# Attention with heads paired on row and column halves, both key tiles projected first, and GpSimd scaling the exponentials by the inverse of their sum

## What is computed

```python
ql, kl, vl = split(xl @ w_qkv + b_qkv)         # 16 heads of 64; 4 key/value heads
ql, kl = apply_rope(ql), apply_rope(kl)        # latents only
for each block of 128 queries:                 # 4 blocks
    keys  = [context 256, window of +-128 around the block]
    logits = (q . k) * 64 ** -0.5, masked to |distance| <= 128
    m = max(max(logits), sink)                 # one sink logit per head
    p = exp(logits - m)
    o = (p / (sum(p) + exp(sink - m))) @ v
```

## Time and profile before

| | us |
|---|---|
| median of three runs | 2054.65 |
| lowest and highest | 2053.88, 2057.94 |
| the profiled execution | 2064.9 |
| its span | 2063.1 |
| TensorE busy | 1968.5 (95%) |

### The profile page before, as it was taken

One profiled execution on the slowest core, in us unless ns is written; L12 is line 12 of the kernel. 1 busy time (PEld: TensorE's weight loads), 2 busy tenths in 40 slices (PEclk: granted clock), 3 DMA queues, 4 the chain that ended last, 5 costly groups with the idle time before them and its releaser, 6 DMA issues.

```text
span 2063.1 us, 26084 instructions
## 1 busy us (share of the span) xinstructions
PE 1968.5 (95%) x10860; PEld 1648.1 (80%) x10860; DVE 1188.6 (58%) x2032; ACT 692.5 (34%) x1053; POOL 22.4 (1%) x18
## 2 busy tenths in 40 slices
PE   4999999999888999999999999999899899999997
PEld 2999999999877888888888888775565578888885
DVE  3456566555763566526552565665255369668485
ACT  3333333333322333213321233345235344233242
POOL 0000000000220000000000000000000000000000
PEclk8999999999998999999999999989989999999998
DMA  6221222112201133323322332110010023233333
GB/s 273 92 76 48 82 82 83 47 67 82 82 1 46 36 130 106 102 96 109 123 89 95 123 112 73 65 42 1 21 41 1 31 80 94 93 102 92 95 100 102
DMA packets 45332, 165.82 MB, mean 80 GB/s; under 512 B 4896, under 2 KB 5280, under 8 KB 45088
## 3 DMA queue, kind: packets, MB, share of 16 engines
q1 hardware_dynamic: 45216, 164.16, 23.8%
HBM read 162.05 MB, written 2.10 MB: 80 GB/s over the span
## 4 chain that ended last, share of the span: by engine, by line
PE 89%; DVE 7%; ACT 2%; DMA 1%; issue 1%; SPq 0%; DVEq 0%
PE slot L390 27%; PE slot L379 8%; PE slot L381 8%; PE slot L380 8%; PE MA L541 4%; PE slot L791 4%; PE slot L792 4%; PE slot L793 4%; PE slot L726 3%; PE MB L448 2%; PE MA L791 2%; PE MA L792 2%; PE MA L793 2%; PE slot L717 2%; PE MB L481 1%; DMA AD<-in_ada 1%
## 5 line engine op out<-in xcount | busy, mean ns | idle before, releaser
L1184 DVE TENSOR_TENSOR WL<-WR,WH 128x1024 fp32r<-128x1024 f32 x204 | 249.4, 1224 | 227.3 <-ACT WH L846 226.2
L846 ACT ACTIVATE WH<-WR 128x1024 fp32r<-128x1024 f32 x204 | 215.4, 1057 | 399.3 <-DMA WR<-in_w 399.3
L379 PE MATMUL slot<-HH,WH 128*128 128x384 f32 (+2 forms) x896 | 324.1, 362 | 24.1 <-DVE HL L1280 11.0
L380 PE MATMUL slot<-HL,WH 128*128 128x384 f32 (+2 forms) x896 | 310.6, 347 | 0.0
L381 PE MATMUL slot<-HH,WL 128*128 128x384 f32 (+2 forms) x896 | 310.5, 347 | 0.0
L379 PEld LDWEIGHTS slot<-HH,WH 128*128 128x128 f32 x896 | 171.0, 191 | 55.0 <-issue 28.7
L390 PE MATMUL slot<-HH,WH 128*128 128x256 f32 (+1 forms) x768 | 199.4, 341 | 2.5 <-DVE ACC L1507 1.6
L390 PE MATMUL slot<-HH,WL 128*128 128x256 f32 (+1 forms) x768 | 196.6, 338 | 0.0
L390 PE MATMUL slot<-HL,WH 128*128 128x256 f32 (+1 forms) x768 | 195.8, 337 | 0.0
L380 PEld LDWEIGHTS slot<-HL,WH 128*128 128x128 f32 x896 | 171.3, 191 | 8.9 <-issue 2.2
L381 PEld LDWEIGHTS slot<-HH,WL 128*128 128x128 f32 x896 | 170.7, 191 | 8.5
(11 more groups left out here) (232 smaller groups left out, 3162.1 us busy)
## 6 DMA issues: line engine op xcount, KB each, us to landing
WR<-in_w SPq DMA_DIRECT2D x204, 512.0 KB, 3.6
ada_raw<-in_ada SPq DMA_DIRECT2D x84, 512.0 KB, 4.6
AD<-in_ada SPq DMA_DIRECT2D x3, 2048.0 KB, 23.6
X<-in_x SPq DMA_DIRECT2D x1, 3072.0 KB, 12.2
out<-Y SPq DMA_DIRECT2D x8, 256.0 KB, 2.2
Y<-in_masks SPq DMA_DIRECT2D x1, 512.0 KB, 19.8
ada_raw<-in_rope SPq DMA_DIRECT2D x1, 512.0 KB, 3.8
small<-in_small SPq DMA_DIRECT2D x1, 327.5 KB, 2.9
```

What stands on the lines that cost most here:

```text
L379: mm(SLOT[s][:, po], WH[w % NB][:, k, :], hi[:, k, to], start=(k == 0), stop=False)
L380: mm(SLOT[s][:, po], WH[w % NB][:, k, :], lo[:, k, to], start=False, stop=False)
L846: go(WH[t % NB][:, :, :], WR[t % NB][:, :, :], ACT.Copy).then_inc(w_hi_done, 1)
L1184: tt(WL[t % NB][:, :, :], WR[t % NB][:, :, :], WH[t % NB][:, :, :].bitcast(F32), ALU.subtract).then_inc(w_split, 1)
```

## The change

Both key tiles are projected first, then all 64 units are worked off in 32 pairs: a pair is the two heads of a query tile, one on TensorE's upper 64 rows and one on the lower.

- **Scores.** The six products of one head alternate with those of the other, one head into MB, the other into MA. The mask's products are gone.
- **Values.** Four pairs share a block of queries; for each chunk the product for the upper four heads (output partitions 0 to 63) is followed by that for the lower four. They are issued in portions of two chunks behind the turns.
- **Maximum.** One VectorE operation per unit (`tensor_tensor_reduce`, two instructions) reads the scores from PSUM, adds a bf16 mask from SBUF (`edge`), writes the scaled negative into PB in SBUF, and gives the minimum with the sink.
- **Exponential.** ScalarE works in place in PB, which has one more column for the sink, so the sum has the sink in it. The small sink exponential and VectorE's addition are gone.
- **Scaling.** VectorE inverts the sum; GpSimd multiplies PB by it and also fills the sink's column. PB has seven buffers, where it had three.
- **Turns.** Chunks 0 to 3 of the two heads go to the two banks of slot 0, the fifth to slot 1. Each is copied from its own place.
- **Rotation.** TensorE's product is gone. VectorE shuffles partitions (`stream_shuffle`), the sine table carries the sign, and ScalarE rounds the high part.

PT and three PB lie where HH and HL were, the rope table and four PB in the space of the weights of the modulation rows.

```diff
+        with ExitStack() as s:
+            PT = [[sb(f"PT{i}{b}", [P, 4, 4, P], F32, s) for b in range(2)] for i in range(2)]
+            PT5 = [sb(f"PT5{i}", [P, 4, 2, P], F32, s) for i in range(2)]
+            PB = [sb(f"PB{i}", [P, 5 * P + 1], F32, s) for i in range(3)]
...
+        with ExitStack() as s:
+            rope = sb("rope", [P, 2, LAT], F32, s)
+            PB += [sb(f"PB{i}", [P, 5 * P + 1], F32, s) for i in range(3, 7)]
...
-        UNITS = [(bi, half, r) for bi in range(LAT // P) for half in range(2) for r in range(4)]
+        UNITS = [(i, bi, r, half) for i in range(2) for bi in range(LAT // P) for r in range(4) for half in range(2)]
+        PAIRS = len(UNITS) // 2
+        BLOCKS = PAIRS // 4
+        LEAD = 2
+        NPB = len(PB)
...
+            def sink_columns():
+
+                pool.wait_ge(nsink_ready, 1)
+                for u in range(len(UNITS)):
+                    i, bi, r, part = UNITS[u]
+                    hd, n = i * 8 + part * 4 + r, chunks(u)
+                    if u >= NPB:
+                        pool.wait_ge(p_turned, u - NPB + 1)
+                    pool.tensor_scalar(PB[u % NPB][:, n * P:n * P + 1], nsink[:, hd:hd + 1], 1.0, 0.0, ALU.mult, ALU.add).then_inc(sink_col, 1)
+                    if u >= 3:
+                        scaled_probs(u - 3)
+                for u in range(len(UNITS) - 3, len(UNITS)):
+                    scaled_probs(u)
+
+            def scaled_probs(u):
+
+                n = chunks(u) * P
+                pool.wait_ge(rden_ready, u + 1)
+                pool.tensor_scalar(PB[u % NPB][:, 0:n], PB[u % NPB][:, 0:n], rden[u % 4][:, :], 1.0, ALU.mult, ALU.mult).then_inc(probs_scaled, 1)
+
+            pool.wait_ge(tile_done, T_AT + 12)
+            sink_columns()
...
-            def rotate(b, s, back=0):
-
-                pe.wait_ge(evacuated[s], tile.half(back))
-                rot.add()
-                pe.wait_ge(roped, rot.now(1))
-                mm(MA[:, 0:LAT], rotm[:, :], RAW[b][:, :], start=True, stop=True).then_inc(rot_done, 1)
...
+            def at_projections():
+
+                first_tiles(TOK, LAT)
+                third_tile(LAT)
+                full_tile(1, LAT, HH, HL)
+                full_tile(0, LAT, HH, HL)
+                full_tile(1, TOK, HH, HL)
+                full_tile(0, TOK, HH, HL)
+                pe.wait_ge(evacuated[1], tile.half(1))
+                value_turns(MB)
+                for j in range(4):
+                    full_tile((j + 1) % 2, LAT, HH, HL)
+                full_tile(1, TOK, HH, HL)
+
+            def at_scores_of(k):
+
+                i, bi, r, _ = UNITS[2 * k]
+                pe.wait_ge(roped, 5 * i + 2 + r)
+                if k >= 1:
+                    pe.wait_ge(row_max, 2 * k)
                 first, n = window(bi)
+                q = slice(bi * P, (bi + 1) * P)
+                lat = slice(CTX + first * P, CTX + (first + n) * P)
+                for po, to in ((slice(PC0, PL0), slice(0, CTX)), (slice(PL0, PL0 + n * P), lat)):
+                    for e, (a, b) in enumerate(((QH, KH), (QH, KO), (QO, KH))):
+                        for part, S in enumerate((MB, MA)):
+                            hp = slice(64 * part, 64 * part + 64)
+                            last = mm(S[:, po], a[i][hp, r, q], b[i][hp, to], start=(e == 0), stop=(e == 2))
+                last.then_inc(at_scores, 2)
-                    mm(S[:, PL0:PL0 + n * P], a[hp, r, q], b[hp, CTX + first * P:CTX + (first + n) * P], start=(e == 0), stop=False)
-                for e, (at, which) in enumerate(edges):
-                    last = mm(S[:, PL0 + at * P:PL0 + (at + 1) * P], tri[:, 2, :], tri[:, which, :], start=False, stop=(e == len(edges) - 1))
-                last.then_inc(at_scores, 1)
...
+                if chunks(u) == 5:
+                    if u % 4 == 0 and fifths(u):
+                        pe.wait_ge(last_ready, fifths(u))
+                    at = (2 * (r % 2) + part) * P
+                    last = turn(SLOT[1][:, at:at + P], PB[u % NPB][:, 4 * P:5 * P], ident[:, :])
...
+                for c in cs:
+                    for part in range(2):
+                        hp = slice(64 * part, 64 * part + 64)
+                        probs = PT[v % 2][part][:, c, :, :] if c < 4 else PT5[v % 2][:, :, part, :]
+                        last = mm(SLOT[1][hp, 512:1024], AV[i][:, at[c], hp], probs, start=(c == 0), stop=(c == n + 1))
+                if cs[-1] == n + 1:
+                    last.then_inc(pv_done, 1)
...
+                for k in range(PAIRS):
+                    if k + LEAD < PAIRS:
+                        at_scores_of(k + LEAD)
+                    at_turn(2 * k)
+                    at_turn(2 * k + 1)
+                    if k >= 4:
+                        v, n = k // 4 - 1, chunks(8 * (k // 4 - 1))
+                        cs = ((0, 1), (2, 3), (4,), ())[k % 4][:max(0, n - 2 * (k % 4))]
+                        if cs:
+                            at_values(v, cs)
...
-                go(PB[u % 3][:, 0:n * P], S[:, PC0:PC0 + n * P], ACT.Exp, scale=AT_SCALE, bias=nm[u % 2][:, :], accum_out=den[u % 4][:, :]).then_inc(probs_ready, 1)
-                go(es[u % 4][:, :], nsink[:, hd], ACT.Exp, scale=-1.0, bias=nm[u % 2][:, :]).then_inc(sink_ready, 1)
...
+            def at_exp(u):
+
+                n = chunks(u) * P + 1
+                act.wait_ge(row_max, u + 1)
+                act.wait_ge(sink_col, u + 1)
+                go(PB[u % NPB][:, 0:n], PB[u % NPB][:, 0:n], ACT.Exp, scale=-1.0, bias=nmax[u % 4][:, :], accum_out=den[u % 4][:, :]).then_inc(probs_ready, 1)
...
+                go(PT[v % 2][part][:, :, r, :], SLOT[0][:, 512 * part:512 * part + 512].rearrange("p (c q) -> p c q", q=P), ACT.Copy).then_inc(pt_ready, 1)
+                if chunks(u) == 5 and u % 4 == 3:
+                    go(PT5[v % 2][:, r - 1:r + 1, :, :], SLOT[1][:, 0:512].rearrange("p (r h q) -> p r h q", r=2, h=2), ACT.Copy).then_inc(last_ready, 1)
...
+            def rope_sums(n):
+
+                b = n % 2
+                i, j = n // 5, n % 5
+                dve.wait_ge(evacuated[j % 2], (T_AT + 6 * i + j) // 2 + 1)
+                link(nc.vector.stream_shuffle(ROT[:, :], RAW[b][:, :], SWAP))
                 mark(tt(RAW[b][:, :], RAW[b][:, :], rope[:, 0, :], ALU.mult))
-                mark(tt(ROT[:, :], MA[:, 0:LAT], rope[:, 1, :], ALU.mult))
+                mark(tt(ROT[:, :], ROT[:, :], rope[:, 1, :], ALU.mult))
                 settle()
-                link(tt(RAW[b][:, :], RAW[b][:, :], ROT[:, :], ALU.add))
-                link(cp(hi, RAW[b][:, :]))
-                tt(lo, RAW[b][:, :], hi.bitcast(F32), ALU.subtract).then_inc(roped, 1)
...
-                    mark(nc.vector.tensor_reduce(mx[u % 2][:, :], (MB, MA)[u % 2][:, PC0:PC0 + n * P], AX.X, ALU.max))
-                w = u - 2
-                if w >= 0:
-                    dve.wait_ge(sink_ready, unit.times(1, (w + 1)))
-                    mark(tt(den[w % 4][:, :], den[w % 4][:, :], es[w % 4][:, :], ALU.add))
...
-                    link(nc.vector.reciprocal(rden[w % 2][:, :], den[w % 4][:, :]))
-                    n = 2 + window(UNITS[w][0])[1]
-                    ts(PB[w % 3][:, 0:n * P], PB[w % 3][:, 0:n * P], rden[w % 2][:, :], None, ALU.mult).then_inc(probs_scaled, 1)
...
+            def masked_max(u):
+
+                i, bi, r, part = UNITS[u]
+                hd, n = i * 8 + part * 4 + r, chunks(u)
+                dve.wait_ge(at_scores, u + 1 + (u + 1) % 2)
+                if u >= NPB:
+                    dve.wait_ge(p_turned, u - NPB + 1)
+                if u >= 4:
+                    dve.wait_ge(probs_ready, u - 3)
+                nc.vector.tensor_tensor_reduce(PB[u % NPB][:, 0:n * P], (MB, MA)[part][:, PC0:PC0 + n * P], edges(bi), -AT_SCALE,
+                                               nsink[:, hd:hd + 1], ALU.add, ALU.min, nmax[u % 4][:, :]).then_inc(row_max, 1)
+
+            def inverse_sum(u):
+
+                dve.wait_ge(probs_ready, u + 1)
+                if u >= 4:
+                    dve.wait_ge(probs_scaled, u - 3)
+                nc.vector.reciprocal(rden[u % 4][:, :], den[u % 4][:, :]).then_inc(rden_ready, 1)
...
+                for k in range(PAIRS):
+                    for u in range(2 * k + 2, min(2 * k + 4, len(UNITS))):
+                        inverse_sum(u)
+                    for u in range(2 * k + 2 * LEAD, min(2 * k + 2 * LEAD + 2, len(UNITS))):
+                        masked_max(u)
+                    if k % 4 == 3 and k > 4:
+                        at_evac(k // 4 - 1)
+                at_evac(BLOCKS - 1)
```

More of the change, by code:

```diff
@@ L712, in at_turn, with value_turns @@
-            def at_turn(u, bi, half, r):
-                pe.wait_ge(probs_scaled, unit.times(1, (u + 1)))
-                if u >= 1:
-                    pe.wait_ge(pt_ready, unit.times(1, u))
-                for c in range(2 + window(bi)[1]):
```

(35 more changed lines are left out.)

257 lines of the change are left out of this document (115 added, 142 removed).

## The result

The changed kernel takes 1955.15 us (median of 4 runs, 1952.8 to 1955.79) where the kernel before takes 2056.3 in the same comparison (2053.88 to 2061.73): ratio 0.951, 95% interval 0.9496 to 0.9525. That is 101 us less; forecast were 88 less and 1967. It lies inside the range, 12 us under the forecast.

The account below looks back on a forecast made before the run. TensorE was taken to bound the kernel until the chain through VectorE's maximum takes over. Projections 83 plus attention 140 gave 223 us for 310.8, 88 less, so 1967 us; range 1950 to 2012.

Parts of the forecast that it names:

- What bounds: Whole stretch: TensorE decides, and taking products off it pays until a chain of the other engines takes over.
- Values on two column halves: Attention values: column halves overlap nearly fully, so eight units take 4.44 us with five chunks, 3.56 with four.
- Scores on two row halves: Attention scores: a pair costs what one unit does, 1.07 or 0.91 us; upper bound 1.95 or 1.62.
- The first rival: Attention: row halves run in sequence (some 20 us) or the maximum costs twice (about 25 us); 1987 to 1995 us; chance 0.2.
- Turns: Attention turns on TensorE: unchanged at 0.69 us a unit with five chunks, 0.59 with four.
- The chain: Attention, pairs without values: copies, exponentials, inverse, maxima, scores and turns take 7.0 us for two pairs, 6.0 with four chunks.
- The doubled one: Masked maximum on VectorE at twice its cost: 5 or 4.2 us a pair, about 25 us in all.
- GpSimd: 64 softmax scalings: 0.69 to 1.28 us each for 640 columns, covered by 2 us to spare in the chain.
- hand-over: Further hand-over for GpSimd's scaling between inverse and turn: 0.1 us a pair, 3 us.
- Fill, end, clock: Attention's ends: 5.5 us before the first turn, 4.4 plus 2.3 at the end, 8 for low clock.
- Projections: Both projections: 83 us, before 101.5, with ten rotations (8.5 us) and the 5.10 us wait for WL gone.
- The clock's rival: Attention loop at the lower clock: 39 us for half of it, 78 for all; 2006 or 2045 us; chance 0.2.

Follow-up runs that it names:

- h1: Changed kernel with the lower four heads' value products sent to the same 64 columns as the upper's; 1983.77 us, stretch +30.0 us.
- h2: Changed kernel with both heads of a pair reading the upper 64 rows for their scores; 1986.73 us, stretch +28.0 us.
- i4: Changed kernel with VectorE making each masked maximum two times over; 1996.7 us, stretch +40.2 us.
- h3: Changed kernel with GpSimd multiplying each PB once more, by one, ahead of its scaling; 1958.5 us, stretch +0.2 us.
- i2: Changed kernel with last query tile's rounding and an early one-column exponential (table load) put ahead of the copy of AVT; 1956.37 us, stretch -1.2 us.
- g3: Changed kernel with ten spare float32 products of 512 columns where the ten rotations stood; 1964.55 us, stretch +7.6 us.
- h4: Changed kernel with the scaling back on VectorE behind each inverse, GpSimd keeping the sink's column; 1961.65 us, stretch +5.1 us.
- g1: Changed kernel with all value products of the upper four heads issued before the lower four's in each portion; 1957.21 us, stretch +1.9 us.
- g2: Changed kernel with one head's six score products issued before the other head's six; 1965.0 us, stretch +8.2 us.

## Why the prediction was right, and by how much it was off

**What bounds.** Right: TensorE paid for what was taken off it, until the chain through the maximum took over in the pairs without values.

**Values on two column halves** (4.44 us for eight units of five chunks): measured 1.87 a portion up to the next scores, 0.94 a chunk, 4.7 for five. h1 shows the cause.

**Scores on two row halves** (1.07 and 0.91 a pair): measured 1.07 and 0.9; the upper bound of 1.95 is what h2 has. The first rival's rows condition was false, and its price of 20 us was near what h2 costs without the clock, 23.

**Turns** (1.38 and 1.18 a pair): 1.24 and 1.03, a little cheaper.

**The chain** (7.0 us for two pairs of five chunks): 6.67. Two maxima take 1.70 for 1.90 and the turns 1.24 for 1.38; the other links are within 0.1. The masked maximum, taken at 0.85 + 0.10, is 0.88 with its neighbour 0.81 behind. The doubled one was priced at about 25 us and cost 40. Its 5 and 4.2 us a pair were near (4.89 and 4.18 in i4), but sixteen of each are 147 us, 30 and not 25 above the 117 of the forecast's loop, and 38 above the 109.3 that the loop really takes; i4's loop is 145.7. The rest is the fill.

**GpSimd** (0.69 to 1.28 a scaling, 2 us to spare, 3 us of hand-over): 0.80 and 0.70, the spare time is there (h3), the 3 us are not. No lock beside VectorE shows: GpSimd's mean stays at 803 ns with maxima beside it, in each of which one input is from PSUM.

**Fill, end, clock.** The end is 6.7, as forecast. The fill is 8.0 for 5.5. I summed the steps of pair 0 alone, but with a lead of two the first turn stands behind the scores of pairs 1 and 2 in TensorE's order: 3.74 us to the scores of pair 1, 2.65 to those of pair 2, 1.58 for these at the lower clock. The first unit was scaled by 1403.00, 1.6 us before its turn. The first maximum also stood behind QO (1398.18), which waited for the rounding on ScalarE; the table load of 1.28 us ended just before that maximum and so added nothing. The low clock, 8 us in the sum, is only at the seam of fill and loop (1402.95 to 1406.3) and costs some 1.5 us, by i2's scores and turns at 1.00. The kernel before had some 38 us of its two attentions at the lower level (mean clock 0.93 over 101.84 us, 0.89 over 107.50).

**Projections** 83.1 for 83; the rotations are 7.5 for 8.5 (g3). No wait for WL is left. The projections are 18.4 us shorter than before; these 7.5 and the wait of 5.10 have their cause in a run and a row; the other 5.8 were not taken apart.

The mechanism held, and the size was 16 us short in the attention, 123.9 for 140. By terms: the loop's blocks, summed as 117, are 109.3. Of that 3.5 is the five-chunk blocks (15.03 and 14.21 for 15.5), and 3.9 the last block: I counted eight full blocks, but behind the last two pairs no scores are left to make or to wait for (9.8 us for 13.7). The hand-over is 3 less, the low clock 8 less as a term of its own, the fill 2.5 more: -7.7 - 3 - 8 + 2.5 = -16. The forecast's stretch of 223 less 16 is 207.

The clock's rival has a sum that does not come out: 26 and 21 us for 15.5 and 13.7 are 71 us over the whole loop, and half of that 36, not 78 and 39.

**What the runs account for.** h1, h2, g3 and h4 give back 30.0, 28.0, 7.5 and 5.1 us, 71 of the 104. No run shows the other 33. By rows they hold the wait for WL (5.10), the mask's products (64 at 0.12 us, some 8, an estimate), one beginning and one end in place of two, and most of the 38 us at the lower clock, of which up to half was lost. These overlap, and no run tells them apart.

## What to carry to other kernels

Products that fill half of TensorE's rows or columns are worth pairing: the pair costs what one does, and the order between the halves may slip by four records at no cost (g1), while six cost 0.32 us (g2) and eight 1.8. Once the pairing has made TensorE cheap, look for the single buffer that ties it to another engine (here MB and MA, freed by the maximum): doubling that engine's step 64 times cost 40 us (i4), while doubling one off that chain (GpSimd's scaling, h3) cost 0.2. Count first and last blocks by what they really contain before multiplying, and read effects of 5 us in the stretch that was edited, not in the span; and look at the clock there too, since i2 and h4 each owe it 1 to 2 us.

## What the runs showed of the hardware

- TensorE started a product on one row half ahead of three that were issued before it on the other (g2), so its order of starts is not the program's between halves.
- In h2 the granted clock stayed at 0.50 (1.2 GHz) for 27 us, with TensorE wholly busy from 1408 on with scores on 64 rows and turns, and rose 0.2 us ahead of the first values. With scores on both halves (the change) it was back at 1.00 (2.4 GHz) after 3.4 us, also during turns, and stayed there with TensorE busy for 2.2 to 3.2 of 4 us. The Trainium skill (TensorE: Matmul & The Clock Gate, Part 4: PE-mode transpose) says that transposes don't count as work for the clock. Both runs have the same turns; the edit to the scores between them made the difference, how is open, and no run here has turns alone.
- In i4, where TensorE waits up to 2.72 us for the maximum, the clock fell to 0.50 six times in the loop; in the change, with waits up to 1.84 us, it fell once, in the fill. Not every long wait was followed by a fall: behind the 2.18 us at 1484.93 the clock stayed at 1.00.
